# A decoder trunk on one Trainium2 core: attention probabilities turned by VectorE in 32x32 blocks and regrouped through main memory, in place of 128x128 turns by TensorE

## The reference, cut to what matters

```
xn = rms_norm(x)
proj = xn @ w_in            # split into pool, q, k, v, spatial gating, convolution
q, k = rope(q), rope(k)     # 8 heads of 64
yb = attention(q, k, v)     # 256 tokens are one block: causal softmax(q k^T / 8) v
ya, yc, yd = pooling, spatial gating unit, convolution module
merged = sum over 4 branches of sigmoid(xn @ w_gate + b) * (y @ w_proj)
x = x + merged @ w_o ;  x = x + SwiGLU(rms_norm(x))
```

## Time and profile before

| what | us |
|---|---|
| median of 3 runs (797.38 to 797.59) | 797.4 |
| the profiled execution | 797.46 |
| its span, first to last instruction | 795.7 |
| TensorE busy in the span | 788.1 |
| VectorE busy | 618.3 |
| ScalarE busy | 436.6 |
| GpSimd busy | 146.8 |

### The profile page before, as it was taken

The page is one execution under the profiler, slowest core; times in us unless marked ns, Lnnn a source line. Parts: engine busy times, 40 slices in busy tenths (PEclk is TensorE's granted clock), DMA queues, the critical chain, the costliest instruction groups (busy, mean ns, idle before and its releaser), DMA issues.

```text
span 795.7 us, 15715 instructions
## 1 busy us (share of the span) xinstructions
PE 788.1 (99%) x6567; PEld 765.4 (96%) x6567; DVE 618.3 (78%) x761; ACT 436.6 (55%) x568; POOL 146.8 (18%) x148
## 2 busy tenths in 40 slices
PE   8999999999999999999999999999999999999997
PEld 8999999999999999999999999999999999999996
DVE  6899999776886766575698899988678767676764
ACT  6766887544654353434465678765356444434434
POOL 2415763074000000000000466513300000000000
PEclk9999999999999999999999999999999999999999
DMA  9975555456645666646568555544646465656541
GB/s 296 306 242 170 182 172 177 159 170 234 219 144 184 208 207 209 209 163 211 170 201 266 159 168 185 180 160 159 212 159 212 160 204 181 218 195 205 185 159 53
DMA packets 118187, 152.23 MB, mean 191 GB/s; under 512 B 3904, under 2 KB 101778, under 8 KB 118128
## 3 DMA queue, kind: packets, MB, share of 16 engines
q1 hardware_dynamic: 116592, 149.30, 57.7%
q0 software_dynamic: 1360, 1.82, 0.8%
q10 hardware_dynamic: 176, 0.27, 0.1%
HBM read 148.23 MB, written 1.05 MB: 188 GB/s over the span
## 4 chain that ended last, share of the span: by engine, by line
PE 99%; DMA 0%; DVE 0%; ACT 0%; issue 0%; DVEq 0%; ACTq 0%
PE bank L974 28%; PE bank L975 28%; PE bank L976 28%; PE bank L1062 3%; PE bank L1064 3%; PE bank L1065 3%; PE bank L1036 1%; PE bank L1035 1%; PE bank L1034 1%; PE bank L1196 1%; PE bank L1176 1%; PE bank L1022 0%; PE bank L1021 0%; PE bank L1023 0%; PE bank L1152 0%; PE bank L1148 0%
## 5 line engine op out<-in xcount | busy, mean ns | idle before, releaser
L974 PE MATMUL bank<-act,w_hi 128*128 128x256 f32 x1472 | 408.5, 278 | 1.0 <-DVE w_lo L1752 1.0
L975 PE MATMUL bank<-act,w_hi 128*128 128x256 f32 x1472 | 406.6, 276 | 0.0
L976 PE MATMUL bank<-act,w_lo 128*128 128x256 f32 x1472 | 406.6, 276 | 0.0
L1400 DVE TENSOR_TENSOR w_lo<-raw,w_hi 128x2048 fp32r<-128x2048 f32 x135 | 315.4, 2338 | 101.9 <-ACT w_hi L648 100.9
L648 ACT ACTIVATE w_hi<-raw 128x2048 fp32r<-128x2048 f32 (+3 forms) x146 | 265.2, 1824 | 133.4 <-PE bank L976 105.7
L974 PEld LDWEIGHTS bank<-act,w_hi 128*128 128x128 f32 x1472 | 276.4, 188 | 2.2 <-issue 1.7
L975 PEld LDWEIGHTS bank<-act,w_hi 128*128 128x128 f32 x1472 | 276.4, 188 | 0.5
L976 PEld LDWEIGHTS bank<-act,w_lo 128*128 128x128 f32 x1472 | 276.4, 188 | 0.0
L974 PE MATMUL bank<-y_hi,w_hi 128*128 128x256 f32 x288 | 79.7, 277 | 0.0
L976 PE MATMUL bank<-y_hi,w_lo 128*128 128x256 f32 x288 | 79.5, 276 | 0.0
L975 PE MATMUL bank<-y_lo,w_hi 128*128 128x256 f32 x288 | 79.5, 276 | 0.0
(11 more groups left out here) (248 smaller groups left out, 996.0 us busy)
## 6 DMA issues: line engine op xcount, KB each, us to landing
raw<-in_w_ffn_in SPq DMA_DIRECT2D x44, 1024.0 KB, 5.0
raw<-in_w_gate SPq DMA_DIRECT2D x32, 1024.0 KB, 5.3
raw<-in_w_ffn_out SPq DMA_DIRECT2D x22, 1024.0 KB, 4.8
raw<-in_w_in SPq DMA_DIRECT2D x18, 1024.0 KB, 6.7
raw<-in_w_o SPq DMA_DIRECT2D x8, 1024.0 KB, 5.0
raw<-in_w_proj_b SPq DMA_DIRECT2D x4, 1024.0 KB, 4.8
raw<-in_w_in SPq DMA_DIRECT2D x12, 256.0 KB, 5.9
gates<-qk SPq DMA_DIRECT2D x32, 64.0 KB, 5.7
```

Of the source, the lines that this page charges most:

```text
L974: nc.tensor.matmul(o, whi, ahi, start=first, stop=False, skip_group_check=skip)
L975: nc.tensor.matmul(o, whi, alo, start=False, stop=False, skip_group_check=skip)
L976: return nc.tensor.matmul(o, wlo, ahi, start=False, stop=last, skip_group_check=skip)
L1400: V.tensor_tensor(lo, raw[slot][:, :], hi.bitcast(F32), ALU.subtract).then_inc(lo_ready[slot], 1)
```

## The change

The six 128x128 turns of a head pair on TensorE and the two copies behind them on ACT are gone. In their place DVE turns the whole 128x768 array of the pair in one instruction that turns each 32x32 block by itself (`V.transpose`, two steps after ATT[hp]). SP writes the array to a scratch in main memory in one transfer, waits for its landing, and reads it back in four transfers of 32 partitions each, which put the blocks where they belong. The columns of `probs` are interleaved in runs of 32, and the product with `v_sb` reads its moving operand in such runs. The tables move: scores at steps 10, 12, 14, 17 (before 10, 13, 16, 19), products with v at 17, 17, 22, 22 (before 16, 19, 21, 22), the pooling matmul at 14 (before 13); taps of the convolution are dealt out anew, 31 as before on either side. Four semaphore waits on transfers stand ahead of the products.

```diff
-ATT = (10, 13, 16, 19)
-PT_AT = (13, 16, 19, 21)
-PV_AT = (16, 19, 21, 22)
-PV_BANK = (3, 2, 4, 6)
-FOLD_AT, POOL_AT, POOL_BANK = 10, 13, 0
+ATT = (10, 12, 14, 17)
+PV_AT = (17, 17, 22, 22)
+PV_BANK = (3, 0, 4, 6)
+PT_DMAS = 4
+FOLD_AT, POOL_AT, POOL_BANK = 10, 14, 0
-TAPS = {7: 1, 9: 1, 11: 2, 12: 2, 13: 1, 14: 4, 15: 3, 16: 3, 17: 4, 18: 4, 19: 3, 20: 3}
+TAPS = {7: 1, 9: 1, 11: 2, 12: 1, 13: 3, 14: 1, 15: 4, 16: 3, 17: 3, 18: 4, 19: 4, 20: 4}
-ACT_TAPS = {7: 4, 8: 4, 9: 2, 10: 2, 13: 4, 14: 3, 15: 3, 16: 3, 17: 3, 18: 3}
+ACT_TAPS = {7: 4, 8: 4, 9: 2, 10: 2, 13: 3, 14: 2, 15: 3, 16: 4, 17: 3, 18: 4}
...
+        turned = [part(trig[:, :, :], 0, [6 * P]), part(gates[:, 26:29, :], 0, [6 * P])]
+        probsT = [part(sq[:, :, :], 6 * P, [6 * P]), part(gates[:, 8:11, :], 0, [6 * P]),
+                  part(gates[:, 29:32, :], 0, [6 * P]), part(sq[:, :, :], 6 * P, [6 * P])]
...
+        def head_blocks(t, i):
+
+            return t.rearrange("p (b c i k) -> p i c b k", c=3, i=2, k=32)[:, i, :, :, :]
...
+            def move_blocks(l, hp):
+
+                sp.wait_ge(blocks_turned, l * HP + hp + 1)
+                sp.dma_start(prob_blocks[l][hp], turned[hp % 2]).then_inc(pt_out[hp], 16)
+                sp.wait_ge(pt_out[hp], 16 * (l + 1))
+                if hp == 1:
+                    sp.wait_ge(pooled_ready, l + 1)
+                if hp == 3:
+                    sp.wait_ge(pv_done, l * HP + 1)
+                for b in range(4):
+                    sp.dma_start(probsT[hp][32 * b:32 * b + 32, :].rearrange("k (a y) -> k a y", a=4),
+                                 prob_blocks[l][hp].rearrange("(a k) (b y) -> b k a y", a=4, b=4)[b])\
+                        .then_inc(pt_in[hp], 16)
...
+                    if u - 7 in ATT:
+                        move_blocks(l, ATT.index(u - 7))
...
-                if u in PT_AT:
-                    hp = PT_AT.index(u)
-                    for i in range(2):
-                        act.wait_ge(pt_done, l * 2 * HP + 2 * hp + i + 1)
-                        copy(probsT[:, i, :], bank[6 + i][:, 0:3 * P]).then_inc(bank_free[6 + i], 1)
...
+                    pe.wait_ge(pt_in[hp], 16 * PT_DMAS * (l + 1))
...
-                        nc.tensor.matmul(o[:, 0:S], v_sb[:, 0, c0:c0 + HEAD_DIM], probsT[:, i, 0:2 * P],
+                        nc.tensor.matmul(o[:, 0:S], v_sb[:, 0, c0:c0 + HEAD_DIM], keys[:, 0:2, :, :],
...
-                if u in PT_AT:
-                    hp = PT_AT.index(u)
-                    pe.wait_ge(probs_ready, l * HP + hp + 1)
-                    for i in range(2):
-                        bank_wait(l, 6 + i, f"PT{hp}")
-                        for c in range(3):
-                            last = nc.tensor.transpose(bank[6 + i][:, c * P:(c + 1) * P], probs[:, i, c * P:(c + 1) * P],
-                                                       ident[:, :])
-                        last.then_inc(pt_done, 1)
...
+                if u - 2 in ATT:
+                    hp = ATT.index(u - 2)
+                    dve.wait_ge(probs_ready, l * HP + hp + 1)
+                    if l or hp > 1:
+                        dve.wait_ge(pt_out[(hp + 2) % HP], 16 * (l + (hp > 1)))
+                    V.transpose(turned[hp % 2], probs).then_inc(blocks_turned, 1)
```

More of the change, by code:

```diff
@@ L216, in build @@
         swish_t, glu_t = conv_a, yd_f
-        probs = part(sq[:, :, :], 0, [2, 3 * P])
-        probsT = part(sq[:, :, :], 6 * P, [2, 3 * P])
+        prob_blocks = [[nc.dram_tensor(f"prob_blocks{l}{hp}", [P, 6 * P], F32).ap() for hp in range(HP)] for l in range(L)]
+        probs = part(sq[:, :, :], 0, [6 * P])
+        turned = [part(trig[:, :, :], 0, [6 * P]), part(gates[:, 26:29, :], 0, [6 * P])]
+        probsT = [part(sq[:, :, :], 6 * P, [6 * P]), part(gates[:, 8:11, :], 0, [6 * P]),
+                  part(gates[:, 29:32, :], 0, [6 * P]), part(sq[:, :, :], 6 * P, [6 * P])]
         conv_n = part(sq[:, :, :], 12 * P, [TT, 256])
@@ L322, in build @@
         probs_ready = sem("probs_ready")
-        pt_done = sem("pt_done")
+        blocks_turned = sem("blocks_turned")
+        pt_out = [sem(f"pt_out{hp}") for hp in range(HP)]
+        pt_in = [sem(f"pt_in{hp}") for hp in range(HP)]
         pv_done = sem("pv_done")
@@ L791, in misc @@
                     for i in range(2):
-                        for q, (a, b) in enumerate(((0, P), (P, 3 * P))):
+                        scores = bank[4 + i][:, 0:3 * P].rearrange("p (c b k) -> p c b k", c=3, k=32)
+                        for q, cs in enumerate((slice(0, 1), slice(1, 3))):
                             c = 2 * q + i
-                            last = nc.scalar.activation(probs[:, i, a:b], bank[4 + i][:, a:b], ACT.Exp, scale=SCALE,
-                                                        bias=nmx[:, c:c + 1], accum_out=den[:, c:c + 1])
+                            last = nc.scalar.activation(head_blocks(probs, i)[:, cs, :, :], scores[:, cs, :, :], ACT.Exp,
+                                                        scale=SCALE, bias=nmx[:, c:c + 1], accum_out=den[:, c:c + 1])
                         last.then_inc(bank_free[4 + i], 1)
@@ L800, in misc @@
                     for i in range(2):
-                        for q, (a, b) in enumerate(((0, P), (P, 3 * P))):
+                        for q, cs in enumerate((slice(0, 1), slice(1, 3))):
                             c = 2 * q + i
-                            last = nc.scalar.activation(probs[:, i, a:b], probs[:, i, a:b], ACT.Copy,
-                                                        scale=rden[:, c:c + 1])
+                            o = head_blocks(probs, i)[:, cs, :, :]
+                            last = nc.scalar.activation(o, o, ACT.Copy, scale=rden[:, c:c + 1])
                     last.then_inc(probs_ready, 1)
@@ L1593, in misc @@
                     conv_taps(l, w0, w0 + TAPS[u])
-                if u in PV_AT:
-                    hp, b = PV_AT.index(u), PV_BANK[PV_AT.index(u)]
+                for hp in [hp for hp in range(HP) if PV_AT[hp] == u]:
+                    b = PV_BANK[hp]
                     lo_of(y_lo[:, 2 + hp, :], bank[b][:, 0:S], y_hi[:, 2 + hp, :], 3 + hp, l).then_inc(bank_free[b], 1)
```

22 lines of the change are left out of this document (10 added, 12 removed).

## The result

| | before | changed |
|---|---|---|
| median of 6 runs, us | 797.44 (797.38 to 798.9) | 791.97 (791.62 to 793.38) |
| profiled execution's span, us | 795.7 | 790.2 |
| TensorE busy, us | 788.1 | 782.6 |
| VectorE busy, us | 618.3 | 620.6 |
| ScalarE busy, us | 436.6 | 431.3 |

The ratio is 0.9936, with a 95% interval of 0.9925 to 0.9946: faster by 5.1 us by the ratio and by 5.5 by the medians. The forecast was 792.6 with a range of 792.0 to 795.5; the median lies 0.03 us under the stated low end, and two of the six runs above it. So the direction and the mechanism came out, and the gain was larger than the 4.84 us of the sum by some 0.6 us.

A forecast was written before the change was run, and what follows sets the result against it. TensorE, busy 788.1 of 795.7 us and never waiting after the start, was taken as the bound. 797.46 - 4.84 (turns) + 0 + 0 = 792.6 us; forecast 792.0 to 793.3 at 0.63, range 792.0 to 795.5 at 0.83.

The forecast's parts named there:

- the case below 792.0: Whole kernel: time under 792.0 us because the units may run smoother with fewer mixed matmuls; chance 0.03.
- The turns: TensorE, attention: removing 48 turns, read from start to start, saves 2.42 us a layer, 4.84 us in two.
- The order of the small work: TensorE between units: five interruptions before and after, 0.10 us each for the switch, so the term is nought.
- VectorE in time: VectorE, attention: a step-by-step ledger claimed its results come before TensorE needs them, so nothing is added.
- The two places that counted: VectorE, attention: first product's low part freeing bank 3 for unit 19, 1.8 us to spare; last convolution tap, 1.65.
- The rival in which the turn gets longer beside GpSimd: VectorE gives a part back: +0.55 us a turn, 793.7, up to 795; chance 0.20 shared with late transfers.
- 4 (x - 1) - 1.65: VectorE's delay a layer for turns of x us; reaches the 2.42 us gain at a turn of 2.0 us.
- The price per turn: VectorE: one 128x768 turn costs 970 ns by the slope over columns, taken as 1.0 us.
- a price by groups of partitions: VectorE rival: turn costs 3.4 us, kernel 808.5; chance 0.05 together with other slower causes.
- The strided operand: TensorE's products with v: runs of 32 cost nought; rival up to +6.5 us, 799.1, chance 0.05.
- The transfers: SP's write and reads: median 5.7 us to landing, pair 3 has 3.3 us to spare; far-late rival 0.04.
- My break-even of 8.55 us a leg: SP, pair 3: with write and reads at 8.55 us each, TensorE's 2.42 us wait eats a layer's gain.

The follow-up runs named there:

- the kernel with three turns: Changed kernel with every turn on VectorE done three times, 16 more turns than in the changed kernel: 800.44 us.
- the kernel with the memset: Changed kernel with one waited-for VectorE memset of an unused column added per layer, ahead of the turn of head pair 2: 791.56 us.
- the packed version: Changed kernel with the products' moving operand read packed instead of in runs of 32, so products take wrong keys' probabilities: 791.9 us.
- the one with four writes: Changed kernel with the write of head pair 3 done four times instead of once, each waited for: 792.98 us.

## Why the prediction was right, and where its sizes were off

The path was right: TensorE is the bound, the turns come off it, and VectorE and the transfers stay inside their spares. The value was not: 792.0 to 793.3 was given 0.63, and the measured 791.97 falls just into the case below 792.0, which was given 0.03. The reason named for that case, that the units run a little smoother with fewer mixed matmuls, is near to what was found, but was not in the sum.

**The turns.** 4.84 us were read from start to start; leaving them out of the kernel before gave 5.0. The step holds.

**The order of the small work.** Here is the term that was mis-sized. I put it at nought by counting interruptions, five before and five after. The count was right, but what an interruption costs depends on what stands in it. What follows a product starts 0.70 us after it if it is a product too, and 0.81 us otherwise (twice a layer, 0.22), and the turn of the convolution alone needs no switch ahead of it (0.09) and takes 0.36 us where it took 0.41 behind a product (0.05). These rows make 0.36 us a layer. The price of 0.10 for an interruption was too low as well, since it covers only the way in: the way back costs 0.1 too, which did not matter with the count unchanged. By TensorE's starts the attention stretch of a layer takes 75.03 us in the changed kernel, 75.48 in the kernel before without turns (70.45 to 145.93) and 77.95 before. So 2.47 us a layer are the turns and 0.45 the order, of which 0.09 are spread over starts that I did not add up: 5.84 in two layers.

**What came back.** 0.39 us were lost outside the stretch (312.62 for 312.23 us between the two stretches), by the one late step of VectorE in the feed-forward part of layer 0. The sum is then 5.84 - 0.39 = 5.45, and the runs show 5.5. The forecast did not have this term and could not have had it from the rows. That the sum came within 0.6 us is thus helped by two terms of opposite sign that it did not hold.

**VectorE in time.** The two places that counted came close: last tap 136.6 for 136.75, low part of the first product 119.3 for 120.1. In between the ledger is off by more and in both directions: step 17 ends at 121.75 for 122.95, and step 18 then takes 5.9 us where 4.85 were put down. That the last tap fits to 0.15 us is therefore in part luck. TensorE never waits for VectorE in the attention stretch. The two tight places were the right ones there, as the kernel with three turns shows; a third lay in the feed-forward part, where the low part is ready only 0.2 us ahead even without the late step (250.07 for 250.25 in the kernel with the memset). The spare before the taps, 1.65 us, is 1.5. The rival in which the turn gets longer beside GpSimd falls with the turns of 0.97 us beside a working GpSimd. What failed was the price of going past it: 4 (x - 1) - 1.65 made a turn of 2.0 us the break-even, while at 1.95 the kernel still is 4.1 us faster than before. VectorE's other work gets shorter when it is shifted against GpSimd, which a ledger of fixed durations does not show. With turns of about 3 us the rival does come true (800.4).

**The price per turn.** The row of 970 ns settles it for the slope over the columns, and against a price by groups of partitions: 128 partitions cost no more than 32. The Trainium skill (VectorE: DVE Perf Modes, The three transpose paths) would have given 1.87 us for the six blocks, an estimate from its price for bf16, and the trace has half of that. The error is in the multiplication, not in the page's 311 ns: the kernel before turns 128 columns in 302 ns,

```profile
L1708 DVE STREAM_TRANSPOSE wsT<-ws_nat 32x128 f32<-32x128 f32 x16 | 4.8, 302 | 0.5
```

and six of these count the fixed part of 0.17 us six times, which one instruction over 768 columns pays once. The advice in the same page's Rules for kernel authors, TensorE for a full 128x128 turn, did not hold in this kernel, where TensorE is never idle and the detour over main memory fits into spare time.

**The strided operand.** Nought was right, and the packed version shows it. By the note on cachelines in the Trainium skill (SBUF — State Buffer, Door 1: The DMA port swizzle) nothing was to be added; the experiment agrees.

**The transfers.** I had 5.7 us for each leg. The write took 5.9 to 10.3, since it stands behind loads of 1 MB (the same write takes 2.3 with none ahead), the reads 1.9 to 3.5, issued when the write has landed and with only each other ahead. Together 8.8 by the medians for 11.4: the cover was thicker than worked out, 6.6 us in layer 0 and 4.0 in layer 1 for 3.3. My break-even of 8.55 us a leg was too kind in another way: with the clock's fall a wait of 2.2 us costs 3.9, so that a wait that size is already more than the gain of a layer. The loads behind the waiting SP, which I had covered by 2 us and more, cost TensorE nothing in the changed kernel and 0.5 us in the one with four writes.

## What to carry to other kernels

When one engine is busy from end to end and waits for nobody, work taken off it is worth its distance from start to start, and the neighbours that it had matter as much as the number of interruptions. Before moving the work to the engine that is nearly as busy, write its steps down against the moments at which the first engine wants each result: the smallest differences (here a bank that must be free two units later, and the last tap) are the spare, and they say more than its share of busy time. List them over the whole span and not only where the change is: the only wait that it brought stood 100 us behind the attention stretch. A ledger of fixed durations was good enough inside the spare here, with errors of up to 1.2 us that partly cancelled, and overstated what lay beyond it, because two engines got out of each other's way.

## What the runs showed of the hardware that I had not expected

A wait of TensorE of 2.2 us was followed by 3.7 us at a granted clock of 0.53; waits of 1.1 us (VectorE's turns twice) and of 1.25 to 1.72 us (three times) left it at 1.00, with matmuls 0.11 us apart again at once. So in these traces a wait of 2.2 us costs 3.9 us and one of 1.7 us little more than itself.

One step of VectorE's program starts 1.16 us after the one before it in the changed kernel, in all of its traces, and 0.79 us in the kernel before and in kernels with one, four or eight instructions more a layer on VectorE. The memset shows that it is not the turn's work but the instructions that stand ahead in the program, since one of no use removes it; what makes it so (a fetch of instructions is one possibility) was not tried and stays open.

A write of 384 KB to main memory lands after 2.3 us with nothing ahead of it in the queue and after 5.5 or more behind a load of 1 MB; a read of 96 KB after 2.2. The row of the four additional writes a layer (the longest is the first, behind a load):

```profile
DMA to landing us min/median/max: 2.3/2.3/5.7
```

VectorE's turn of 128x768 costs 0.97 us beside a working GpSimd as well, while the subtraction of 128x2048 goes from 2.28 to 2.83 us there.
